# Where selection operations, gating, maximum passes and reciprocals stand in VectorE's stream

## The chip, the cores and the metric

One core of a Trainium2 chip runs the whole kernel. TensorE multiplies matrices, VectorE and ScalarE work on elements, GpSimd works on elements more slowly, SyncE issues the DMAs. Every engine runs its own list of instructions in the order in which the program wrote it; semaphores make one engine wait for another. The metric is the time of the whole program on the device in microseconds (us), as a median of several runs. A difference below some 0.2% can't be told from none.

## The reference

Two decoder layers over 1040 tokens (16 meta tokens and 1024 of the sequence, width 1024). A layer projects its input once, runs four branches of eight heads each, multiplies each by a gate, projects back and normalises:

```python
def hybrid_layer(x, ...):
    h = split_cols(x @ w_in)
    out_a = causal_dense_attention(qa, ka, va, key_valid, HEAD_DIM ** -0.5, decay)
    out_b = mla_attention(h['b_cq'], h['b_ckv'], h['b_kr'], ...)
    out_c = dsa_sparse_attention(...)      # keys chosen by an indexer
    out_d = sliding_window_sink_attention(...)
    mixed = jnp.concatenate([out_a * jax.nn.silu(h['a_g']), out_b * jax.nn.silu(h['b_g']),
                             out_c * jax.nn.silu(h['c_g']), out_d * jax.nn.silu(h['d_g'])], axis=-1)
    return layer_norm(ALPHA * x + mixed @ w_out, ln_g, ln_b)

def dsa_sparse_attention(...):             # for each block of 128 queries
    score = jnp.einsum('bqhk,bqh->bqk', jax.nn.relu(s), iwb) * IDX_HEADS ** -0.5
    _, idx = lax.top_k(jnp.where(adm, score, NEG), 256)
    # softmax attention over the 256 chosen keys alone
```

All arithmetic is in float32.

## The kernel before, in words

**Tiling.** Queries go in nine blocks: block 0 holds the 16 meta tokens, blocks 1 to 8 hold 128 tokens each. Block `i` sees `keys_of(i)` = 16 + 128 i keys: 1040 for block 8, 912 for block 7, 272 for block 2. Heads go in pairs, `p` = 0 to 3 in each branch. The order of a layer is an indexer stage, then branches A, D, B, C with four pairs each, then the output stage. Below, "pair A1" is pair 1 of branch A, and **step** `idx` of a pair works on block 8 - `idx` (the list `ORDER`, line 31), so step 0 is the largest block and step 8 the smallest. There are 2 x 16 x 9 = 288 steps.

**The plan.** The class `Plan` writes one list of items, and each engine goes through this one list and emits its own share of each item. So the order in which `pair` (line 318) adds items is the order of every engine's work; there is no other scheduler. A step adds, in this order: `tri` or `near` (GpSimd prepares the mask of the last chunk, A and C only), `rec` of the step before (`normalise`, line 386), `qk` part 0 (scores of this step's first two chunks), `pv` with the values of a block pair (`values`), `tp` of the step two before (`probabilities`, transposes), `qk` part 1 (third chunk), `exp` for the first head, `top` (line 395), `gt` (`gated`, line 396), a tile of projection work, `tp` for the second head, `exp` for the second head, and more projection work.

**What the items do.**
- `qk`: TensorE writes a chunk of scores for both heads into PSUM banks of `ps_s` (L980, in B also the rotary part, L991). VectorE's **maximum pass** (L1362) adds mask or bias, writes the row to `arena` and keeps the negative maximum in `nmax`; its end (semaphore `max_done`) frees the banks. Two pairs of banks, 0/1 and 2/3, take turns (`next_slot`).
- `exp`: ScalarE turns the row into exponentials and adds them up (L1148).
- `rec`: VectorE takes the **reciprocal** of the sums (L1374; in D, L1373 adds the sink first), then GpSimd multiplies the row by it (L1457, `nrm_done`). VectorE waits here for both exponentials of the step.
- `tp`: TensorE transposes the probabilities (L1003) into two banks of `ps_t`; ScalarE copies them out (L1159), and in C VectorE copies every other group (L1326).
- `pv`: TensorE multiplies values (L1015) into the single bank `ps_o`, in steps 1, 2, 4, 6 and 8.
- `gt`: VectorE's **gating** (L1382) multiplies `ps_o` by the gate tile, frees `ps_o` (`o_free`), and SyncE stores the result. VectorE waits here for `pv_done`.
- `mt` with what = "G", in steps 0 to 2: a chunk of the next gate tile. TensorE (L936) writes bank `P_BANK` = 4, ScalarE takes tanh (L1116) once `o_free` says that the old gate has been read, VectorE multiplies (L1299) and frees the bank. Other `mt` chunks are copied by ScalarE (L1109, L1112).
- `qb` (L945): a chunk of B's next queries, also in bank 4. For the rotary ones (what = "R") VectorE runs a chain of four instructions (L1312, L1314, L1316, L1317) before the bank is free. They fall in steps 6 and 7 (two in 7) of B0 to B2, and in steps 7 and 8 of D3.
- `kb` (L951): the three chunks of B's keys, added by `k_latent` in step 8 of D3 and of B0 to B2; ScalarE copies them (L1120).
- `top`: **selection operations** of VectorE on the indexer's scores, `TOP_OPS` = 448 per layer: for each block 8 down to 2, 64 operations over its whole row. They alternate: a maximum of eight (`MAX8`, L1193) and a replacement of these eight (`MATCH_REPLACE8` after `MATCH_VALUE_LOAD`, L1195). After the last of a block L1199 and L1200 make the mask. C needs all masks. `TOP_RATE` (line 43) says how many a step takes: 5 in A, 3 in D, 4 in B. That makes 432; the other 16 are done by line 1339, in the VectorE part, ahead of the first maximum pass of C.

```python
if br == "C" and it["p"] == 0 and it["idx"] == 0:
    top_ops(TOP_OPS)
```

Of the kernel before, what the change touches and what calls it, by code (L numbers as in the profile page):

```python
# [35 lines left out]
P_BANK = 4  # L36
# [3 lines left out]
Y_PARTS = [(0, 2), (2, 4), (4, 6), (6, 8), (8, 10), (10, 16)]  # L40

W_OUT_SETS = [4, 3, 3, 3, 3]
TOP_RATE = {"A": 5, "D": 3, "B": 4, "C": 0}


def keys_of(i):
    return N_META + BLK * i
# [6 lines left out]
def rows_of(b):  # L54
    return N_META if b == 0 else BLK
# [9 lines left out]
def score_chunks(br, i):  # L65

    if br == "D":
        return [(0, min(keys_of(i), 2 * BLK))]
    n = keys_of(i)
    if br == "C":  # L70
        tail = n if i <= 2 else 2 * BLK
        main = n - tail
        return (even(main, 1 if main <= 512 else 2) if main else []) + [(main, tail)]
    if br == "B":
        return [(0, 512), (512, 512), (1024, 16)] if n > 1024 else even(n, 2 if n >= 272 else 1)
    return even(n, -(-n // 512))
# [60 lines left out]
class Plan:  # L137
# [101 lines left out]
                for what in "NR" for c in range(3)]  # L239

    def k_latent(self, l, p):
        for c, bank in enumerate((P_BANK, 0, 2)):
            self.add("kb", l=l, p=p, cols=CHUNKS[c], **self.group("act", bank))

    def layer(self, l):
# [72 lines left out]
    def pair(self, l, br, p, nxt):  # L318

        fill = {}  # L320
        put = lambda idx, work: fill.setdefault(idx, []).append(work)
        for idx, work in enumerate(self.tile(l, "G", br=br, p=p)):
            put(idx, work)
        if br == "A":
            if p + 1 < NP:
                rest = self.tile(l, "AQ", p=p + 1) + self.tile(l, "AK", p=p + 1)
            else:
                rest = self.tile(l, "K", br="D") + self.tile(l, "Q", br="D", p=0)
            for idx, work in zip((3, 4, 5, 6, 7, 7), rest):
                put(idx, work)  # L330
        elif br == "D":
            if p + 1 < NP:
                for idx, work in zip((3, 4, 5), self.tile(l, "Q", br="D", p=p + 1)):
                    put(idx, work)
                for idx, b in zip((6, 7, 8), range(3 * p, 3 * p + 3)):
                    put(idx, lambda b=b: self.token_block(l, "TB", b))
                    if b:
                        put(idx, lambda b=b: self.latent(l, b - 1))
            else:
                put(0, lambda: self.latent(l, NB - 1))  # L340
                put(0, lambda: self.add("uw", l=l))
                work = [lambda b=b: self.token_block(l, "VB", b) for b in range(NB)]
                for idx, fn in zip((3, 3, 4, 4, 5, 5, 6, 6, 7, 4, 5, 6, 7, 8, 8), work + self.q_latent(l, 0)):
                    put(idx, fn)
                put(8, lambda: self.k_latent(l, 0))
        elif br == "B":
            if p + 1 < NP:
                for idx, work in zip((3, 4, 5, 6, 7, 7), self.q_latent(l, p + 1)):
                    put(idx, work)
                put(8, lambda: self.k_latent(l, p + 1))  # L350
            else:
                rest = self.tile(l, "K", br="C") + self.tile(l, "Q", br="C", p=0)
                for idx, work in zip((3, 4, 5, 6, 7, 7), rest):
                    put(idx, work)
        elif p + 1 < NP:
            for idx, work in zip((3, 4, 5), self.tile(l, "Q", br="C", p=p + 1)):
                put(idx, work)
        else:

            yy = self.take("yy")  # L360
            self.y_parts = self.y_half(l, ORDER[0], yy, 0) + self.y_half(l, ORDER[0], yy, 1)
            put(5, lambda: self.add("yl", l=l, b=ORDER[0], yy=yy, ln=None))
            for idx in (7, 8):
                put(idx, lambda: self.y_parts.pop(0)())

        hu = 8 * l + (p if br == "D" else 4 + p) if br in "CD" else None
        for idx, i in enumerate(ORDER):
            st = self.take("st")
            chunks = []
            for c0, w in score_chunks(br, i):  # L370
                g = self.take("chunk")
                bank = self.next_slot()
                chunks.append(dict(c0=c0, w=w, bank=bank, g=g,
                                   waits=self.banks([bank, bank + 1], ("max_done", 2 * (g + 1)))))
            row = (NB - 1 - i) % 3
            owner = self.row_owner[row]
            n = min(keys_of(i), 2 * BLK) if br == "D" else keys_of(i)
            s = dict(l=l, br=br, p=p, i=i, st=st, idx=idx, n=n, M=rows_of(i), chunks=chunks, row=row,
                     rwaits=latest([owner] if owner else []), a=(i + 1) // 2, hu=hu,
                     ds=self.take("ds") if br == "D" else None, tri=self.take("tri") if br == "A" else None,  # L380
                     nb=self.take("nb") if br == "C" else None)
            if br == "A":
                self.add("tri", **s)
            if br == "C":
                self.add("near", **s)
            self.normalise()
            self.add("qk", part=0, **s)
            self.values()
            self.pending.append(s)
            old = self.pending.pop(0) if len(self.pending) > LAG else None  # L390
            self.probabilities(old, 0)
            if len(chunks) > 2:
                self.add("qk", part=1, **s)
            self.add("exp", e=0, **s)
            self.add("top", l=l, count=TOP_RATE[br])
            self.gated()
            work = fill.get(idx, [])
            for fn in work[:1]:
                fn()
            self.probabilities(old, 1)  # L400
            self.add("exp", e=1, **s)
            for fn in work[1:]:
                fn()
            self.rec_next = s
        return None
# [49 lines left out]
def latest(events):  # L455
    out = {}
    for name, v in events:
        out[name] = max(out.get(name, 0), v)
    return sorted(out.items())
# [1098 lines left out]
```

## Time and profile before

| what | value |
|---|---|
| median of 3 runs | 3426.13 us (3424.23 to 3426.8) |
| the profiled execution | 3431.51 us, its span 3429.6 us |
| granted TensorE clock, mean | 0.964 of full speed |
| TensorE (PE) busy | 3117.4 us, 91% |
| VectorE (DVE) busy | 1701.0 us, 50% |
| ScalarE (ACT) busy | 1023.9 us, 30% |
| GpSimd (POOL) busy | 549.2 us, 16% |

"Busy" is the time in which an engine executes; an engine that is not busy waits for a semaphore or has nothing to do. The chain that ended last, followed back from the end, is made of the output stage's matmuls (L1029) for 6% of the span. In the trace an instruction stands with its start from the beginning of the span; TensorE's weight loads (PEld) run beside its matmuls. A float32 matmul is recorded as two instructions.

### The profile page before, as it was taken

Reading aid. Unit: us, or ns where it says so; the run is one execution under the profiler, and the core shown is the slowest. Engines: PE = TensorE matmul, PEld = TensorE weight load, DVE = VectorE, ACT = ScalarE, POOL = GpSimd, SP = SyncE. Lnnn points to the kernel's source line nnn. Section 1 sums busy time; section 2 is a strip of 40 time slices with the busy share of each in tenths; the row PEclk is TensorE's granted clock in tenths of the full one; section 3 lists DMA queues with packets and bytes.
Section 4 is the critical chain, followed back from the end, with each engine's and each line's share of the span. In section 5 each row is a group of like instructions: output and inputs, shape, how many; then the busy total and the mean of one; then the engine's idle time right before and its main releaser. Section 6 shows DMA issues by size and latency. Waiting matters only on the chain. (4 is left out here: it accounts for less than half of the span.)

```text
span 3429.6 us, 39909 instructions
## 1 busy us (share of the span) xinstructions
PE 3117.4 (91%) x14214; PEld 1769.8 (52%) x14214; DVE 1701.0 (50%) x4511; ACT 1023.9 (30%) x2757; POOL 549.2 (16%) x994
## 2 busy tenths in 40 slices
PE   4999999999799989989998998899998989899898
PEld 3445555555455555544443455555554555555443
DVE  4225877755566543432121268777555664443222
ACT  1223333334334323320002233333434443233100
POOL 0000222111111123320000012221111111333100
PEclk8999999999899999999999999999999999999999
DMA  5000110110000002032210001101110000120321
GB/s 210 27 25 26 38 38 28 35 36 28 32 15 20 15 27 93 19 128 67 74 59 21 25 31 38 38 28 36 35 42 19 15 15 19 31 87 13 117 74 61
DMA packets 91003, 153.04 MB, mean 45 GB/s; under 512 B 12656, under 2 KB 68224, under 8 KB 88504
## 3 DMA queue, kind: packets, MB, share of 16 engines
q1 hardware_dynamic: 90808, 150.50, 13.3%
q8 instruction: 115, 1.88, 0.2%
q14 instruction: 80, 0.66, 0.1%
HBM read 120.36 MB, written 32.21 MB: 44 GB/s over the span
## 5 line engine op out<-in xcount | busy, mean ns | idle before, releaser
L936 PE MATMUL ps_s<-xT,w_ring 128*128 128x348 f32 (+2 forms) x3616 | 1154.9, 474 | 11.0 <-DVE gate L1299 8.6
L936 PEld LDWEIGHTS ps_s<-xT,w_ring 128*128 128x128 f32 x3616 | 685.8, 195 | 415.0 <-issue 125.6
L1457 POOL TENSOR_SCALAR arena<-arena,small 128x256 f32<-128x256 f32 (+9 forms) x576 | 361.2, 638 | 1667.4 <-DVE small L1374 1663.2
L1148 ACT ACTIVATE arena<-arena,small 128x256 f32<-128x256 f32 (+9 forms) x576 | 380.2, 660 | 261.8 <-DVE small L1362 261.2
L1003 PE MATMUL ps_t<-ident,arena 128*128 128x128 f32 (+2 forms) x2432 | 361.0, 277 | 67.4 <-ACT arena L1159 49.6
L1159 ACT ACTIVATE arena<-ps_t 128x512 f32<-128x512 f32 (+4 forms) x700 | 309.4, 471 | 367.7 <-PE ps_t L1003 359.1
L1193 DVE MAX8 small<-score 128x8 f32<-128x1040 f32 (+6 forms) x448 | 377.3, 842 | 10.2
L980 PE MATMUL ps_s<-feat 64*128 64x256 f32 (+12 forms) x1888 | 318.9, 440 | 63.3 <-DVE small L1362 57.9
L1003 PEld LDWEIGHTS ps_t<-ident,arena 128*128 128x128 f32 (+2 forms) x2432 | 256.0, 132 | 228.2 <-issue 100.4
L1195 DVE MATCH_REPLACE8 score<-small,score 128x1040 f32<-128x1040 f32 (+6 forms) x448 | 369.8, 825 | 0.0
L1015 PE MATMUL ps_o<-arena 128*64 128x256 f32 (+3 forms) x2816 | 316.9, 362 | 31.5 <-ACT arena L1159 13.6
L1029 PE MATMUL ps_s<-arena,feat 128*128 128x512 f32 (+1 forms) x680 | 304.0, 600 | 10.2 <-DMA arena<-in_w_out 10.2
L1015 PEld LDWEIGHTS ps_o<-arena 128*64 128x64 f32 (+1 forms) x2816 | 181.9, 138 | 165.7 <-issue 55.9
L980 PEld LDWEIGHTS ps_s<-feat 64*128 64x128 f32 (+1 forms) x1888 | 150.8, 185 | 181.5 <-DVE small L1362 79.1
L1029 PEld LDWEIGHTS ps_s<-arena,feat 128*128 128x128 f32 (+1 forms) x680 | 126.5, 187 | 176.0 <-issue 163.8
L1232 DVE SCALAR_TENSOR_TENSOR arena<-score,ps_s 128x512 f32<-128x512 f32 (+1 forms) x34 | 23.3, 686 | 381.7 <-PE ps_s L1029 346.8
L906 PE MATMUL ps_s<-arena,xT 128*128 128x272 f32 (+3 forms) x576 | 202.4, 506 | 9.1 <-DMA arena<-in_w_tc 4.2
L1374 DVE RECIPROCAL small<-small 128x2 f32<-128x2 f32 (+1 forms) x288 | 46.8, 162 | 259.8 <-ACT arena L1148 256.2
L1288 DVE SCALAR_TENSOR_TENSOR score<-arena,small,score 128x1040 f32<-128x1040 f32 (+6 forms) x98 | 88.0, 901 | 175.6 <-ACT arena L1133 169.7
L906 PEld LDWEIGHTS ps_s<-arena,xT 128*128 128x128 f32 (+1 forms) x576 | 103.6, 185 | 96.7 <-issue 78.0
L1299 DVE SCALAR_TENSOR_TENSOR gate<-gate,ps_s 128x348 f32<-128x348 f32 (+1 forms) x96 | 49.3, 513 | 202.0 <-ACT gate L1116 202.0
L1116 ACT ACTIVATE gate<-ps_s 128x348 f32<-128x348 f32 (+1 forms) x96 | 44.1, 459 | 334.5 <-PE ps_s L936 268.5
(125 smaller groups left out, 2361.2 us busy)
## 6 DMA issues: line engine op xcount, KB each, us to landing
w_ring<-in_w_feat SPq DMA_DIRECT2D x78, 512.0 KB, 3.5
mixed<-mixg SPq DMA_DIRECT2D x128, 128.0 KB, 1.7
feat<-mixed SPq DMA_DIRECT2D x16, 1024.0 KB, 6.7
resid<-score SPq DMA_DIRECT2D x16, 512.0 KB, 3.1
score<-resid SPq DMA_DIRECT2D x16, 512.0 KB, 7.5
arena<-in_w_out SPq DMA_DIRECT2D x4, 1536.0 KB, 8.0
cT<-falls SPq DMA_DIRECT2D x8, 520.0 KB, 4.8
feat<-falls SPq DMA_DIRECT2D x8, 520.0 KB, 5.3
```

The costliest lines, as they stand in the source:

```text
L906: mm = pe.matmul(ps_s[0:M, bank, 0:n], xT[:, k, cols], wv[:, k, :], start=(k == 0), stop=(k == KT - 1))
L936: mm = pe.matmul(ps_s[:, bank, 0:w], w_ring[:, wt % 2, k, :], xT[:, k, c0:c0 + w], start=(k == 0), stop=(k == KT - 1))
L980: mm = pe.matmul(ps_s[0:M, ch["bank"] + e, 0:ch["w"]], q[r:r + HD, qc], k[r:r + HD, k0 + ch["c0"]:k0 + ch["c0"] + ch["w"]], start=True, st ...
L1003: mm = pe.transpose(ps_t[0:w, tg % 2, c * BLK:c * BLK + M], p_row(it, h, k0, w), ident[0:M, 0:M])
L1015: mm = pe.matmul(ps_o[HD * e:HD * e + HD, at:at + w], v_of(br, p, e, kb), arena[0:rows_of(kb), src:src + w], start=(j == 0), stop=(j == le ...
L1029: mm = pe.matmul(ps_s[0:M, bank, :], mix_in[slot][:, k, 0:M], w_out[k][:, cols], start=(k == 0), stop=(k == 15))
L1148: nc.scalar.activation(p, p, ACT.Exp, scale=-1.0, bias=nm[:, e:e + 1], accum_out=psums[0:M, st % 4, e:e + 1]).then_inc(S["exp_done"], 1)
L1159: a = nc.scalar.activation(dst, src, ACT.Copy)
L1193: dve.max(top8, sc).then_inc(S["top_step"], 1)
L1195: dve.match_replace(sc, top8, sc, TAKEN).then_inc(S["top_step"], 1)
L1288: dve.scalar_tensor_tensor(sc, src, w, sc, ALU.mult, ALU.add).then_inc(S["acc_done"], 1)
L1457: nc.gpsimd.tensor_scalar(p, p, rinv[0:M, st % 4, e:e + 1], 1.0, ALU.mult, ALU.mult).then_inc(S["nrm_done"], 1)
```

## The change

It has four edits, all in the plan.

1. `TOP_RATE` becomes a list with a number for each step. A pair takes 38 operations in A (before 45), 36 in D (before 27), 38 in B (before 36). In A and B step 8 takes 1.
2. `gated` is called ahead of `top`: in VectorE's stream the gating stands before the step's selection operations instead of behind them.
3. `qk` part 0 is added ahead of `normalise`: in VectorE's stream this step's first maximum passes stand before the reciprocal of the step before.
4. `k_latent` writes its first chunk to the bank pair that the scores used longer ago, the second to bank 4, the third to the other pair. Before: bank 4, 0, 2.

```diff
-TOP_RATE = {"A": 5, "D": 3, "B": 4, "C": 0}
+TOP_RATE = {"A": [3, 4, 5, 5, 6, 4, 5, 5, 1], "D": [4, 4, 4, 4, 4, 4, 4, 4, 4],
+            "B": [4, 4, 5, 5, 5, 5, 5, 4, 1], "C": [0] * 9}
...
     def k_latent(self, l, p):
-        for c, bank in enumerate((P_BANK, 0, 2)):
+        free = 2 * self.slot
+        for c, bank in enumerate((free, P_BANK, 2 - free)):
             self.add("kb", l=l, p=p, cols=CHUNKS[c], **self.group("act", bank))
...
                 self.add("near", **s)
+            self.add("qk", part=0, **s)
             self.normalise()
-            self.add("qk", part=0, **s)
             self.values()
...
             self.add("exp", e=0, **s)
-            self.add("top", l=l, count=TOP_RATE[br])
             self.gated()
+            self.add("top", l=l, count=TOP_RATE[br][idx])
             work = fill.get(idx, [])
```

## Rows read from the trace of the kernel before

**Rows 1.** The page, part 1: busy us, share of the span, instructions of an engine.
```profile
PE 3117.4 (91%) x14214; PEld 1769.8 (52%) x14214; DVE 1701.0 (50%) x4511; ACT 1023.9 (30%) x2757; POOL 549.2 (16%) x994
```

**Rows 2.** Waits of TensorE over the whole run: for whom, us, times, longest.
```profile
PE ps_s L980 <- DVE small L1362: 57.9, 29, 9.4
PE ps_t L1003 <- ACT arena L1159: 49.6, 97, 3.3
PE ps_s L945 <- DVE feat L1317: 29.2, 10, 4.5
PE ps_t L1003 <- DVE arena L1326: 17.6, 26, 1.9
```

**Rows 3.** Windows, steps 0 to 3: six pairs of A, C1, and A0 of layer 1.
```profile
core 0: us, PE busy (x) PEld busy (x) DVE busy (x) ACT busy (x) POOL busy (x), PEclk, DMA share, GB/s
396.70:442.60 45.90, 37.20 (x157) 22.29 (x156) 40.87 (x82) 15.44 (x34) 9.78 (x16) 0.89 0.13 41
...
sum 267.10, PE 219.94 PEld 132.12 DVE 226.37 ACT 92.58 POOL 58.68; mean PE 36.66 PEld 22.02 DVE 37.73 ACT 15.43 POOL 9.78
...
1309.60:1344.80 35.20, 33.12 (x165) 20.50 (x164) 16.53 (x61) 12.43 (x26) 12.11 (x16) 1.00 0.46 179
2012.40:2049.10 36.70, 30.93 (x136) 18.32 (x134) 35.37 (x73) 14.49 (x29) 9.27 (x14) 1.00 0.18 58
```

**Rows 4.** Groups of VectorE instructions in A1's stretch: busy, mean ns.
```profile
L1193 DVE MAX8 small<-score 128x8 f32<-128x1040 f32 (+1 forms) x12 | 14.8, 1232 | 0.3
L1195 DVE MATCH_REPLACE8 score<-small,score 128x1040 f32<-128x1040 f32 x11 | 13.5, 1226 | 0.0
...
L1195 DVE MATCH_VALUE_LOAD score<-small,score 128x8 f32 x11 | 1.0, 91 | 0.3
```

**Rows 5.** Timeline of TensorE in pair A1, idle time and its releaser in brackets.
```profile
401.84 1.52 PE L980 MATMUL ps_s<-feat 64*128 64x344 f32 x4 [3.73 <-DVE small L1362]
...
421.34 0.29 PE L1015 MATMUL ps_o<-arena 16*64 16x16 f32 x4 [2.20 <-ACT arena L1159]
```

**Rows 6.** Waits over the whole run, ScalarE's for the gating.
```profile
ACT gate L1116 <- DVE mixg L1382: 66.0, 12, 6.2
```

**Rows 7.** Windows, step 0 of C0 and of C1, layer 0.
```profile
1232.40:1251.60 19.20, 9.83 (x35) 5.58 (x34) 11.19 (x39) 2.69 (x7) 3.29 (x6) 0.73 0.07 20
1309.60:1317.80 8.20, 7.56 (x35) 4.42 (x34) 3.80 (x14) 2.29 (x7) 1.89 (x4) 1.00 0.90 348
```

**Rows 8.** Timeline of TensorE in the first step of C0.
```profile
1243.36 1.23 PE L980 MATMUL ps_s<-feat 64*128 64x256 f32 x4 [9.37 <-DVE small L1362]
```

**Rows 9.** Waits over the whole run, VectorE's before reciprocal and gating.
```profile
DVE small L1374 <- ACT arena L1148: 256.2, 149, 7.5
...
DVE mixg L1382 <- PE ps_o L1015: 32.1, 18, 3.5
```

**Rows 10.** Timeline of VectorE in pair B1, steps 6 and 7.
```profile
1056.25 0.57 DVE L1193 MAX8 small<-score 128x8 f32<-128x400 f32 x1
...
1059.60 0.52 DVE L1312 SCALAR_TENSOR_TENSOR rtmp<-ps_s,rope_t 64x348 f32<-64x348 f32 x1 [0.49 <-PE ps_s L945]
```

**Rows 11.** Timelines of TensorE in pair B1 (steps 6, 7) and pair D3.
```profile
1054.63 3.17 PE L1015 MATMUL ps_o<-arena 128*64 128x256 f32 x28
...
1066.79 2.15 PE L945 MATMUL ps_s<-cT,vw 128*128 128x344 f32 x4 [3.13 <-DVE feat L1317]
...
922.51 3.83 PE L951 MATMUL ps_s<-cT,vw 128*128 128x348 f32 x6 [2.04 <-DVE feat L1317]
```

**Rows 12.** Groups of selection instructions by shape, rows 400 wide, whole run.
```profile
L1193 DVE MAX8 small<-score 128x8 f32<-128x400 f32 x64 | 36.8, 575 | 1.1
...
L1195 DVE MATCH_REPLACE8 score<-small,score 128x400 f32<-128x400 f32 x64 | 35.8, 559 | 0.0
```

**Rows 13.** Windows: stage D of layer 0, and steps 4 to 8 of A1.
```profile
662.00:927.00 265.00, 238.06 (x1050) 140.35 (x1048) 154.50 (x451) 105.36 (x368) 44.91 (x110) 0.96 0.11 35
442.60:483.10 40.50, 39.49 (x211) 25.11 (x210) 28.75 (x58) 14.12 (x40) 9.31 (x20) 1.00 0.06 20
```

## The prediction

> **What bounds the kernel now.** I read the page's first part before anything else: TensorE is busy for 3117 of 3430 us [rows 1]. Nothing that only moves VectorE work can shorten those 3117 us, except where TensorE ran them at its lower clock; the change can win the idle time between matmuls and the slow matmuls beside it. The second view is who TensorE waits for [rows 2]: for VectorE's maximum passes (57.9 us), for ScalarE's copies of transposed probabilities (49.6 us), for the rotary chain that empties the one projection bank (29.2 us), for VectorE's own transposed copies (17.6 us). The third view cuts the run into equal pieces of work. Steps 0 to 3 (blocks 8 to 5) of a head pair have nearly the same matmuls in branch A and in branch C, but only A has selection operations between them. Six such stretches of A (pairs A1 to A3 in both layers) take 267.1 us, 44.5 each, at a granted clock of 0.89 in the first; the one of C takes 35.2 us at 1.00 [rows 3]. So A's first four steps are where VectorE sets the pace.
>
> **Why A is slow.** Two chains show in pair A1. Step 8 gives TensorE 3 us of work and VectorE five selection operations of 1.28 us (one maximum 1.232, or a load 0.091 and a replacement 1.226 [rows 4]). They run into the next pair, its first maximum pass is late, and TensorE stands 3.73 us before its third chunk [rows 5]. Then in steps 1 and 2 ScalarE's tanh may not overwrite the gate tile before VectorE's gating instruction has read it, and that instruction is behind five selection operations: ScalarE waits 66.0 us in 12 places for it [rows 6], its copies come late behind the tanh, and TensorE waits 2.20 us at the head of step 2 [rows 5]. The engine then works at half its clock (1.2 instead of 2.4 GHz) for a while: 0.89 is the mean over the stretch, and C's stretch without those stops is at full clock [rows 3]. The Trainium skill says the same of such gaps (TensorE: Matmul & The Clock Gate, HAM oscillation); by that rule a removed stop gives back more than its own length, and the trace agrees (0.89 against 1.00).
>
> **Part 1, A's steps 0 to 3.** With step 8 down from 5 operations to 1, step 0 from 5 to 3, step 1 from 5 to 4, and the gating ahead of them, both chains go. What is left is C's time: six stretches are 6 x 35.2 = 211.2, so 267.1 - 211.2 = 55.9 us. Pair A0 has no previous pair; its stretch is 36.7 us with 30.93 busy [rows 3], 5.8 idle, of which I leave 2.3 (first maximum pass and copies): 3.5 per layer, 7 in all. That makes 63. Against it: in A0 and A1 the rows are 1040 wide and VectorE is nearly full. The stretch of A1 has 40.87 us of VectorE work with 23 selection instructions [rows 3, 4]; 17 remain, so 40.87 - 6 x 1.28 = 33.2 us in a stretch of 35.2. I charge 1.5 us for each of these four pairs for being late, 6 us, and take **-57 us**; the bounds are -63 and half, -30.
>
> **Part 2, start of C.** The 16 left-over operations stood, whole, ahead of C's first maximum. The first step of C0 takes 19.20 us with a TensorE stop of 9.37 us [rows 7, 8], the same step of C1 8.20 us [rows 7]; both layers have the same order there, so I count it twice. The new rates add up to 4 x (38 + 36 + 38) = 448, all there are, so none is left, and the mask is ready one step before. 2 x 11.0 = **-22 us**. The cover of those 16 is B and D, below; bounds -22 and -19.
>
> **Part 3, gating ahead of selection: a new wait.** VectorE can now stand before the gating until TensorE has finished the value matmuls, with the selection operations, the gate product or the rotary chain and the next maximum queued behind. The trace of before has this wait only 18 times, 32.1 us [rows 9], since five operations covered it. In A and C nothing urgent is behind. In B, steps 6 and 7, there is: each rotary chain frees the bank for the next query chunk. In B1 the maximum ends at 1056.25, where selection starts; the value matmuls run until 1054.63 + 3.17 = 1057.80, so the gating ends at 1058.2 [rows 10, 11]. Five operations (now 5, not 4) of 0.64 us follow (0.575 for a maximum, 0.091 + 0.559 for a replacement, some 0.03 between them [rows 4, 12]): 3.2 us, so the chain starts at 1061.4 instead of 1059.60 and TensorE's stop of 3.13 us [rows 11] grows, with the one before it, by about 2.0. B0 pays 1.5 (its rows in step 7 shrink from 528 to 400), B2 1.3 (272 wide). 4.8 per layer is 9.6, and I add 3 for a half clock that lasts longer after these stops (the first such stretch of A shows that stops and low clock go together). **+13 us**, bounds 0 and +20. In D, 4 operations instead of 3 are 36 x 0.8 = 29 us per layer in a stage of 265 with 154.5 of VectorE busy [rows 13]: hidden, 0, bounds 0 and +4; if that cover were gone, 58 us. In A's later steps (4 to 8, 40.50 us with 28.75 busy) the waits are hidden likewise [rows 13]. The Trainium skill has a rule against this part (TensorE: Matmul & The Clock Gate, Architectural detail: the array is 16× 32×32, not 1× 128×128): VectorE's queue is strictly first in, first out. By it nothing behind the gating can pass its wait; the trace agrees, as a late gating holds ScalarE's tanh up for 66.0 us while selection runs [rows 6]. If all those waits reached TensorE, it would be the slower rival below.
>
> **Part 4, maximum ahead of the reciprocal.** The reciprocal waits for ScalarE's second exponential, 256.2 us in 149 places [rows 9]; the maximum no longer does. In C, where no selection covers it, the maximum and then VectorE's transposed copies come up to 1 us earlier; TensorE's waits for these are 17.6 us in all [rows 2]. I take a third, 5, and 1 for D3: **-6 us**, bounds 0 and -17.6. What is late next: GpSimd's normalising starts after the maximum (3.3 us at most), but its probabilities are transposed one step later, so no stop; its next bias sum in C queues behind it, in short steps only. ScalarE, SyncE and TensorE have neither reciprocal nor selection in their streams, so nothing else is moved past them, and no DMA.
>
> **Part 5, banks of the latent keys.** The first chunk no longer waits for the rotary chain, 2.04 us once per layer [rows 11], but the second does, and in D3 that chain comes about 1.3 us later (one operation more, and the gating). **0**, bounds -4 and +2.
>
> **Sum.** -57 - 22 + 13 - 6 + 0 = -72 us. The profiled execution took 3431.51 us (span 3429.6, 1.9 around it), 5.4 above the median 3426.13. 3431.5 - 72 = 3359.5 there, and 3354 us as a median.
>
> **Rivals.** *VectorE stays late in A.* 33.2 of 35.2 us leaves 2.0 for waits. If they are more, the 1040-wide pairs stay stretched and half of part 1 is lost: +28, 3382 us. For: the tanh and exponential waits stand in series with this work. Against: at 912 wide (A2, A3) there is room. *The rotary chains cost more.* If the stops of B and D3 double the low clock, part 3 is +20 to +30: 3366. *The stops of A are not these chains'*, so that only C's start comes: 3426 - 22 + 13 = 3417. Against: the releasers named in the rows. *Slower:* the wait before the gating, up to 3.2 us in step 4 and 1.5 in step 6, with half-clock time behind it, is not hidden but pushes every maximum; with about 6.7 us for each of the 24 pairs of A, D and B it costs 161, less the 95 of other gains: 3492 us. It decides from 4 us a pair on. Against: 11.7 us of VectorE idle in A's steps 4 to 8 alone [rows 13].
>
> **How the numbers follow.** Forecast 0.70; VectorE late 0.12; rotary chains 0.10; only C's start 0.04; slower 0.04. Range: 3332 (part 1 whole, part 3 nothing, part 4 at -10) to 3390 (half of part 1, with part 3 at +20). About 0.2% is what a measurement of this kernel can tell from no change. Faster 0.94, same 0.02, slower 0.04.
>
> **What would show it.** After: the six stretches of A near 36 us at clock 1.00; ScalarE's wait for the gating near 0; C0's first step 8.2 us; TensorE's wait for the maximum about 20 us; its wait for the rotary chain up from 29 to about 39; VectorE's wait for the value matmuls up from 32 to over 100 us. The forecast is wrong if A's stretches stay above 39, or if stops of 3 us appear in D.

## The result and the profile after

| | before | after |
|---|---|---|
| median of 4 runs each, taken together | 3426.47 us | 3326.97 us (3320.94 to 3329.28) |
| ratio, 95% interval | 1 | 0.9695 (0.9677 to 0.9712) |
| the profiled execution, its span | 3431.51, 3429.6 us | 3328.77, 3326.8 us |
| granted TensorE clock, mean | 0.964 | 0.978 |

The changed kernel is 3.05% faster: 27 us more than the 72 forecast, and below the range that was given (3332 to 3390). In the changed file a line of the old one stands 4 further down (L980 is L984, L1362 is L1366, L1382 is L1386, L1317 is L1321).

The page after, part 1, against [rows 1]:

```profile
PE 3079.5 (93%) x14214; PEld 1750.7 (53%) x14214; DVE 1690.5 (51%) x4511; ACT 1021.2 (31%) x2757; POOL 551.1 (17%) x994
```

The instructions are the same in number on every engine. TensorE is busy 38 us less with the same instructions, so that is matmuls that run at the higher clock; the other 65 us of the 103 are idle time. Who TensorE still waits for, against [rows 2] (us, times, longest):

```profile
PE ps_s L949 <- DVE feat L1321: 35.7, 16, 4.2
PE ps_t L1007 <- ACT arena L1163: 34.6, 97, 0.6
...
PE ps_s L984 <- DVE small L1366: 24.4, 24, 1.5
PE ps_t L1007 <- DVE arena L1330: 15.6, 27, 1.5
```

The maximum passes went from 57.9 to 24.4 us with no stop above 1.5, ScalarE's copies lost their long stops (longest 3.3, now 0.6), and the rotary chain took first place, 35.7 us in 16 places instead of 29.2 in 10.

**Where the time went.** I cut both runs at the first score matmul of each branch. Rows: layer 0's branches A, D, B, C (C with the output stage), then layer 1's. Columns: stretch and its length, busy us of each engine, granted clock, DMA. Before:

```profile
315.20:662.40 347.20, 314.25 (x1556) 193.72 (x1554) 273.92 (x578) 120.65 (x300) 75.05 (x140) 0.95 0.11 36
662.40:926.90 264.50, 237.56 (x1046) 140.04 (x1044) 154.10 (x450) 105.35 (x368) 44.91 (x110) 0.96 0.11 35
926.90:1232.40 305.50, 282.37 (x1683) 170.00 (x1683) 174.51 (x595) 119.17 (x301) 49.30 (x70) 0.95 0.05 18
1232.40:2012.40 780.00, 735.88 (x2861) 382.42 (x2860) 230.21 (x610) 165.40 (x409) 101.92 (x166) 0.98 0.17 55
2012.40:2356.00 343.60, 310.21 (x1556) 192.24 (x1554) 273.50 (x578) 120.73 (x300) 75.05 (x140) 0.97 0.11 36
2356.00:2620.20 264.20, 237.53 (x1046) 140.25 (x1045) 154.18 (x450) 105.33 (x368) 44.91 (x110) 0.96 0.11 35
2620.20:2922.10 301.90, 278.80 (x1683) 168.56 (x1683) 174.50 (x595) 119.11 (x301) 49.31 (x70) 0.96 0.06 18
2922.10:3429.60 507.50, 462.54 (x1919) 247.73 (x1918) 164.18 (x509) 94.99 (x236) 100.31 (x162) 0.97 0.20 64
```

And after:

```profile
315.60:624.90 309.30, 298.63 (x1556) 185.88 (x1554) 246.77 (x540) 120.05 (x300) 75.14 (x140) 1.00 0.13 40
624.90:886.10 261.20, 235.39 (x1044) 138.79 (x1043) 184.96 (x498) 104.68 (x368) 44.68 (x108) 0.97 0.11 36
886.10:1192.60 306.50, 281.52 (x1682) 169.97 (x1682) 174.54 (x609) 119.56 (x301) 50.24 (x72) 0.95 0.06 18
1192.60:1958.80 766.20, 731.63 (x2859) 380.82 (x2858) 220.67 (x587) 165.34 (x409) 102.02 (x166) 0.99 0.17 56
1958.80:2269.90 311.10, 300.29 (x1558) 186.66 (x1556) 246.91 (x540) 120.21 (x300) 75.16 (x140) 0.99 0.12 40
2269.90:2528.20 258.30, 232.78 (x1044) 137.78 (x1043) 184.93 (x498) 104.63 (x368) 44.69 (x108) 0.97 0.11 36
2528.20:2834.50 306.30, 281.22 (x1682) 169.79 (x1682) 174.58 (x609) 119.53 (x301) 50.23 (x72) 0.95 0.06 18
2834.50:3326.80 492.30, 459.21 (x1919) 245.87 (x1918) 155.22 (x486) 94.05 (x236) 100.42 (x162) 0.99 0.20 66
```

Length less busy time is TensorE's idle time of a stage. The two layers together: A -70.4 us, D -9.2, B +5.4, C with the output stage -29.0; -103.2 in all, against -102.8 in the span. In A idle time falls from 33.0 to 10.7 us in layer 0 while VectorE does 27 us less there and 31 us more in D: the operations moved to where they are covered.

**A's first four steps**, against [rows 3]: the first of the six stretches and their sum, then C1's of layer 0 and A0's of layer 1, and the first step of C0 against [rows 7].

```profile
392.70:426.50 33.80, 32.42 (x159) 19.83 (x158) 32.29 (x70) 15.42 (x34) 9.77 (x16) 1.00 0.18 56
...
sum 202.50, PE 194.20 PEld 118.80 DVE 189.16 ACT 92.29 POOL 58.61; mean PE 32.37 PEld 19.80 DVE 31.53 ACT 15.38 POOL 9.77
```

```profile
1258.20:1293.20 35.00, 33.06 (x167) 20.52 (x166) 16.06 (x61) 12.43 (x26) 12.12 (x16) 1.00 0.47 181
1958.80:1994.00 35.20, 32.55 (x136) 19.14 (x134) 31.77 (x69) 14.47 (x29) 9.29 (x14) 0.95 0.17 61
1192.60:1200.80 8.20, 7.56 (x35) 4.42 (x34) 3.82 (x16) 2.75 (x7) 3.32 (x6) 1.00 0.16 48
```

Of the stops of A1 in [rows 5], the one of 3.73 us at the pair's start is down to 0.65, and the one of 2.20 is gone. A third, at the end of step 2, goes from 2.36 us to 0.31. In TensorE's timeline, before (the stop of 2.36) and after:

```profile
432.25 0.49 PE L1003 MATMUL ps_t<-ident,arena 128*16 128x128 f32 x2 [2.36 <-ACT arena L1159]
```

```profile
394.82 0.85 PE L984 MATMUL ps_s<-feat 64*128 64x344 f32 x4 [0.65 <-DVE small L1366]
417.68 0.39 PE L1007 MATMUL ps_t<-ident,arena 128*16 128x128 f32 x2 [0.31 <-ACT arena L1163]
```

Of the two waits named in [rows 6] and [rows 9], ScalarE's for the gating has vanished (all 96 waits of its tanh are now for TensorE's chunk, 316.0 us, where 84 of them were before, 268.5 us), and VectorE's for the value matmuls grew from 32.1 us in 18 places to:

```profile
DVE mixg L1386 <- PE ps_o L1019: 130.4, 74, 3.5
```

**B1, steps 6 and 7**, against [rows 10, 11]: VectorE's gating and the first rotary instruction, then TensorE's stops.

```profile
1015.27 0.42 DVE L1386 SCALAR_TENSOR_TENSOR mixg<-ps_o,gate 128x256 f32<-128x256 f32 x1 [1.61 <-PE ps_o L1019]
...
1018.78 0.52 DVE L1316 SCALAR_TENSOR_TENSOR rtmp<-ps_s,rope_t 64x348 f32<-64x348 f32 x1
```

```profile
1020.89 1.41 PE L949 MATMUL ps_s<-cT,vw 128*128 128x348 f32 x4 [1.91 <-DVE feat L1321]
1025.97 1.77 PE L949 MATMUL ps_s<-cT,vw 128*128 128x344 f32 x4 [3.12 <-DVE feat L1321]
```

VectorE stands 1.61 us before the gating, then the five operations run, and the chain starts 3.5 us after the gating's start. The second stop is the old one (3.13, now 3.12); a new one of 1.91 us stands ahead of it.

### The profile page after: what moved, and what is told of

Its sections match the earlier page's. It is cut to its first block and busy times, and to the rows that moved or that the text cites. A ratio compares the mean times of both kernels' runs of the same rounds, so it can differ in the third digit from the quotient of the medians.

```text
span 3326.8 us, 39909 instructions
## 1 busy us (share of the span) xinstructions
PE 3079.5 (93%) x14214; PEld 1750.7 (53%) x14214; DVE 1690.5 (51%) x4511; ACT 1021.2 (31%) x2757; POOL 551.1 (17%) x994
## 5 line engine op out<-in xcount | busy, mean ns | idle before, releaser
L940 PE MATMUL ps_s<-xT,w_ring 128*128 128x348 f32 (+2 forms) x3616 | 1139.5, 469 | 5.1 <-DVE gate L1303 2.4
L940 PEld LDWEIGHTS ps_s<-xT,w_ring 128*128 128x128 f32 x3616 | 677.0, 192 | 399.3 <-issue 104.5
L984 PE MATMUL ps_s<-feat 64*128 64x256 f32 (+12 forms) x1888 | 310.2, 430 | 29.2 <-DVE small L1366 24.4
L984 PEld LDWEIGHTS ps_s<-feat 64*128 64x128 f32 (+1 forms) x1888 | 146.8, 180 | 143.5 <-issue 70.2
L1366 DVE CUSTOM_DVE_ANT_0 arena<-ps_s,causal 128x512 f32<-128x512 f32 (+5 forms) x144 | 57.7, 437 | 164.9 <-PE ps_s L995 164.6
L1120 ACT ACTIVATE gate<-ps_s 128x348 f32<-128x348 f32 (+1 forms) x96 | 44.1, 460 | 316.0 <-PE ps_s L940 316.0
L1330 DVE COPY arena<-ps_t 128x384 f32<-128x384 f32 (+4 forms) x124 | 65.2, 528 | 142.6 <-PE ps_t L1007 142.3
```

The costliest lines, as they stand in the source:

```text
L940: mm = pe.matmul(ps_s[:, bank, 0:w], w_ring[:, wt % 2, k, :], xT[:, k, c0:c0 + w], start=(k == 0), stop=(k == KT - 1))
L984: mm = pe.matmul(ps_s[0:M, ch["bank"] + e, 0:ch["w"]], q[r:r + HD, qc], k[r:r + HD, k0 + ch["c0"]:k0 + ch["c0"] + ch["w"]], start=True, st ...
```

## The experiments

A stop is a stretch in which TensorE is idle, and half-clock time is time for which its granted clock is 0.5. Idle times are TensorE's between the cuts described above, layer 0 where none is named. A ratio is to runs of the kernel before on the same chip. Those had a median of 3431.1 to 3433.0 us beside the experiments (single runs from 3424 to 3440), against the 3426.5 of the first table, so a gain is best read from the ratio; where I give one in us it is against the median beside it.

**The edits one by one.** The kernel before with one edit each: the rates and nothing else,

```diff
-TOP_RATE = {"A": 5, "D": 3, "B": 4, "C": 0}
+TOP_RATE = {"A": [3, 4, 5, 5, 6, 4, 5, 5, 1], "D": [4] * 9, "B": [4, 4, 5, 5, 5, 5, 5, 4, 1], "C": [0] * 9}
```

> The kernel before with the new rates alone. Two chains (theory): the late first maximum of A's step 0 and the start of C go, the tanh that waits for the gating in A's step 2 stays. A's six step-0 stops of 2.4 to 3.7 us fall to 0.65, C0's first step falls from 19.2 to 8.1 us, the stops in A's step 2 (4.9, 4.6, 3.6 us) stay within 1 us. Time -45 to -60 us, about 3375. Load alone (rival: VectorE simply had too much to do, order is irrelevant): the stops of step 2 go too, since steps 0 to 2 have three operations fewer; -85 us or more, 3340.

the gating and nothing else,

```diff
-            self.add("top", l=l, count=TOP_RATE[br])
             self.gated()
+            self.add("top", l=l, count=TOP_RATE[br])
```

> The kernel before with the gating ahead of selection alone, old rates. Two chains: the stops of A's step 2 go (20 us a layer with the slow clock behind them), those of step 0 and of C's start stay; B's rotary chains come later by the wait for the value matmuls, +1 us in B1. Time -30 to -42 us, about 3390. Load alone: nothing moves by more than 5 us, since VectorE has the same work.

the maximum passes and nothing else,

```diff
-            self.normalise()
             self.add("qk", part=0, **s)
+            self.normalise()
```

> The kernel before with the maximum ahead of the reciprocal alone. Two chains: it touches neither; a few tenths in C's steps 1 and 2 and 0.7 us in D3, -2 to -8 us. Rival (the maximum's wait for the second exponential is what held A up): -20 us or more.

and the first two together:

> Rates and gating without the two other edits. If they add up, A is as in the changed kernel (309 us in layer 0) and the time is -88 to -96 us, 3334. If the four edits need each other (rival: with the reciprocal first, VectorE has no room in A's 1040-wide pairs), A keeps 5 us or more over that, and the time is above 3342.

| kernel | median us | gain us | ratio, interval | idle in A, layer 0 / 1 |
|---|---|---|---|---|
| before, beside the next four | 3431.13 | | 1 | 33.0 / 33.4 |
| rates | 3374.85 | 56 | 0.983 (0.9806 to 0.9854) | 23.4 / 23.6 |
| gating | 3420.6 | 11 | 0.9967 (0.9954 to 0.9979) | 28.2 / 28.6 |
| maximum | 3405.85 | 25 | 0.9921 (0.9894 to 0.9948) | 28.9 / 29.3 |
| rates and gating | 3342.67 | 88 | 0.9736 (0.9711 to 0.9762) | 12.0 / 12.2 |
| all (after), beside 3426.47 | 3326.97 | 99.5 | 0.9695 (0.9677 to 0.9712) | 10.7 / 10.8 |

The rates came out as expected. The gating alone missed: 3420.6 instead of 3390. The maximum passes alone gave 25 us, where 2 to 8 were expected; that is the rival's figure (20 or more), though A's large stops stayed: in A1 they are 3.75 and 1.98 us, where they were 3.73 and 2.20. In its trace the four branches of both layers lose 24.1 us: A 11.7 (8.1 of it idle, in layer 0 TensorE's waits for ScalarE's copies, 18.5 to 14.4 us), D 9.5, C 6.8, and B gains 3.9. The second trace of the kernel before has A 3.8 us shorter than the first, so the 11.7 are 8 to 12.

Rates and gating together came to what was expected of the two (88 to 96 us), but they are not the sum of what each gives alone: 56 and 11 us alone, 88 together. Pair A1 shows why. With the rates alone, the stop at the start falls to 0.85 us and those behind the gating stay, 0.92 us at the head of step 2 and 4.05 at its end, where 2.20 and 2.36 were (file lines one further down):

```profile
396.36 0.85 PE L981 MATMUL ps_s<-feat 64*128 64x344 f32 x4 [0.85 <-DVE small L1363]
...
423.95 0.59 PE L1004 MATMUL ps_t<-ident,arena 128*16 128x128 f32 x2 [4.05 <-ACT arena L1160]
```

With the gating alone it is the other way round: step 2's stops shrink to 0.85 and 0.31, and the stop at the start of the pair grows from 3.73 [rows 5] to 5.68.

```profile
404.46 1.52 PE L980 MATMUL ps_s<-feat 64*128 64x344 f32 x4 [5.68 <-DVE small L1362]
...
424.70 4.92 PE L936 MATMUL ps_s<-xT,w_ring 128*128 128x348 f32 x16 [0.85 <-DVE gate L1299]
```

VectorE's work is the same, so time that TensorE no longer loses in the middle of a pair leaves VectorE less time to work off its list; it is late at the next pair's start instead. That was then an idea, and the next kernel tests it.

**Is it the load?** The kernel before with the gating ahead, and four of the five operations of A's step 8 sent to D's step 8:

```diff
-TOP_RATE = {"A": 5, "D": 3, "B": 4, "C": 0}
+TOP_RATE = {"A": [5] * 8 + [1], "D": [3] * 8 + [7], "B": [4] * 9, "C": [0] * 9}
```

> The kernel before with the gating ahead of selection, and A's step 8 down from 5 operations to 1 (the 4 go to D's step 8, so that C's start keeps its 16). If the gating alone gained little because VectorE was still late by its load when a pair began, the step 0 stops of 5.68, 5.08 and 4.35 us shrink by four operations (4 x 1.28 = 5.1 us) to under 1 us, A's idle time goes from 28.2 us per layer to about 16, and the time from 3420.6 to 3385 or so. If the five operations in steps 0 to 3 are what keeps VectorE late, stops before the gate's chunk in step 2 take their place: idle about 24 us per layer and 3400 to 3410. If load has no part in it, it stays at 3418 to 3423.

3387.4 us (0.9858, 0.9841 to 0.9874), idle in A 16.9 us: the numbers that the expectation gave if VectorE was late by its load (3385, 16). In A1 the stop at the start went from 5.68 to 0.85 us; five operations in steps 0 to 3 leave 1.56 us in step 2.

```profile
399.38 0.85 PE L980 MATMUL ps_s<-feat 64*128 64x344 f32 x4 [0.85 <-DVE small L1362]
417.93 4.92 PE L936 MATMUL ps_s<-xT,w_ring 128*128 128x348 f32 x16 [1.56 <-DVE gate L1299]
```

So sixteen operations a layer, moved from the one step that could not cover them, release 33 us (3420.6 to 3387.4; 37 by the ratios). They cost something where they went: D's idle time rose from 27.7 to 32.9 us, 3.1 of it in D3, where they stand ahead of a rotary chain (its stop goes from 3.44 to 6.55 us). The move without the gating was not run, so this kernel does not say what each of the two is worth; the gating on top of the new rates is worth 32 us (3374.85 to 3342.67).

**How full may VectorE be?** The changed kernel with the same 38 operations a pair, more of them in steps 0 to 3 (23 instead of 17):

```diff
-TOP_RATE = {"A": [3, 4, 5, 5, 6, 4, 5, 5, 1], "D": [4, 4, 4, 4, 4, 4, 4, 4, 4],
+TOP_RATE = {"A": [5, 6, 6, 6, 3, 3, 4, 4, 1], "D": [4, 4, 4, 4, 4, 4, 4, 4, 4],
```

> The changed kernel with A's 38 operations dealt [5,6,6,6,3,3,4,4,1]: six more in steps 0 to 3, which at 1040 wide is 7.7 us more of VectorE work in a stretch that TensorE passes in 33.7. Theory of the prediction (what VectorE is over, TensorE loses): about 5 to 6 us in each of A0 and A1, 3 in A2 and A3 at 912 wide, with slow clock 40 us in all, 3367. Rival (two pairs of banks and two transposed steps in hand let VectorE be late by several us before TensorE stops): under 10 us, 3335.

3356.05 us (0.9785, 0.9766 to 0.9804), 29 us above the changed kernel: between the two expectations, 40 us and under 10, and nearer to the first. Idle in A 24.1 us. The place where it shows in A1 is not the maximum pass but VectorE's gate product, which has to free the projection bank for the next gate chunk:

```profile
420.19 4.92 PE L940 MATMUL ps_s<-xT,w_ring 128*128 128x348 f32 x16 [2.83 <-DVE gate L1303]
...
430.54 4.92 PE L940 MATMUL ps_s<-xT,w_ring 128*128 128x348 f32 x16 [1.64 <-DVE gate L1303]
```

TensorE's wait for L1303 is 28.0 us over the run here, 2.4 in the changed kernel; with 20 operations in these steps, in the kernel with the light step 8, it is 13.7 (L1299 there). The cover ends gradually between 17 and 23 operations.

**The gating's place in B.** The changed kernel with B's gating behind the selection, as it was:

```diff
-            self.gated()
+            if br != "B":
+                self.gated()
             self.add("top", l=l, count=TOP_RATE[br][idx])
+            self.gated()
```

> The changed kernel with the gating behind the selection again in B alone. Theory: B1's stop in step 7 (5.03 us) falls by the 1.6 us that VectorE waits for the value matmuls less nothing else, to 3.4; B2's likewise by 1, B0's by 0.5: -3 us a layer, -6 in all, 3321. Rival (the fifth operation of step 6 makes it): under 1 us a layer.

3321.74 us (0.9679, 0.9661 to 0.9697), 5 us below the changed kernel, 7 below its runs on the same chip (3328.59); the intervals of the ratios overlap, so the time alone does not show a gain; the idle time is the firmer reading. It falls in B from 25.0 to 21.8 us in layer 0 and from 25.1 to 23.2 in layer 1. The new stop of B1 (1.91) is down to 0.17, the old one stands at 3.12: this is the price of part 3 in B, 2 to 3 us of idle time a layer.

**Selection behind everything in those steps.** In steps 6 and 7 of B0 to B2 and 7 and 8 of D3 the operations go to the end of the step:

```diff
-            self.add("top", l=l, count=TOP_RATE[br][idx])
+            late = (br == "B" and p < NP - 1 and idx in (6, 7)) or (br == "D" and p == NP - 1 and idx in (7, 8))
+            if not late:
+                self.add("top", l=l, count=TOP_RATE[br][idx])
...
             for fn in work[1:]:
                 fn()
+            if late:
+                self.add("top", l=l, count=TOP_RATE[br][idx])
```

> The changed kernel with the selection of steps 6 and 7 of B0 to B2 and of steps 7 and 8 of D3 put behind the rotary chains, at the end of the step. Theory: the chains start when their matmuls end; TensorE's stop of 1.91 us before the second rotary chunk goes and that of 3.1 before the third falls to about 1.4, 3.6 us in B1, 8 in B's three pairs, 2 in D3: 10 a layer, 20 in all with a few us of slow clock, 3305. Rival (the stops of B are the chains' own length, not what stands ahead of them): under 5 us. A loss would mean that the maximum behind the selection is late instead.

It missed: 3325.15 us (0.969, 0.9672 to 0.9709) where 3305 was expected, B's idle time 1.5 us lower per layer. The first rotary chain starts in time now, but step 6's operations stand between it and step 7's, and TensorE's one remaining stop in B1 is 3.74 us. Behind one chain is ahead of the next.

**No selection beside the rotary chains.**

```diff
-            "B": [4, 4, 5, 5, 5, 5, 5, 4, 1], "C": [0] * 9}
+            "B": [6, 6, 6, 6, 6, 6, 0, 0, 2], "C": [0] * 9}
```

> The changed kernel with B's selection operations taken out of steps 6 and 7 and put in steps 0 to 5 (6, 6, 6, 6, 6, 6, 0, 0, 2; the pair still takes 38). If the operations queued ahead of the rotary chains make the stops of B (3.50, 5.03, 3.83 us in step 7), what is left of each is the chain between two rotary chunks of one step, about 1.6 us: 7.5 us less idle per layer, 15 in all, with the half clock behind the stops 20 to 25, so 3303 to 3312 us. The rival is that six operations in steps 0 to 5 make VectorE late there and the gain is given back: B's idle time stays at 25 us per layer and the time within 3322 to 3332.

3296.85 us (0.9601, 0.9586 to 0.9615): 30 us under the changed kernel, and below the 3303 that the first theory had for its lower end. Idle in B 25.0 to 17.8 us, its half-clock time from 28.1 to 6.8 (in layer 1 from 27.8 to 14.1). Each of B0 to B2 keeps one stop of 1.60 us, the wait for the chain between two rotary chunks of one step; six operations a step elsewhere cost nothing that shows.

```profile
1013.71 1.39 PE L949 MATMUL ps_s<-cT,vw 128*128 128x344 f32 x4 [1.60 <-DVE feat L1321]
```

**The rotary chunks one step apart**, in B and D3 and then in B alone, on top of that:

```diff
-                for idx, work in zip((3, 4, 5, 6, 7, 7), self.q_latent(l, p + 1)):
+                for idx, work in zip((3, 3, 4, 5, 6, 7), self.q_latent(l, p + 1)):
...
-                for idx, fn in zip((3, 3, 4, 4, 5, 5, 6, 6, 7, 4, 5, 6, 7, 8, 8), work + self.q_latent(l, 0)):
+                for idx, fn in zip((3, 3, 4, 4, 5, 5, 6, 6, 7, 3, 4, 5, 6, 7, 8), work + self.q_latent(l, 0)):
```

> As the one before, and the chunks of B's next queries stand one step apart where they are rotary: steps 5, 6, 7 in B0 to B2 instead of 6, 7, 7, and steps 6, 7, 8 in D3 instead of 7, 8, 8. If the rest of the stops is a rotary chain between two chunks of the same step, B's stops in step 7 go to under 0.5 us and D3's in step 8 (5.44 and 0.88 us) to about 3 together: some 8 us less idle per layer than the one before, so 3283 to 3295 us. The rival is that the chunks moved ahead wait for ScalarE's latents or for the bank's former user, and the stop only changes its place: then it stays within 5 us of the one before.

> The changed kernel with no selection operations in steps 6 and 7 of B and the rotary chunks one step apart in B alone, D3 as in the changed kernel. If the spreading's gain in B (3.7 us less idle per layer than without it) was given back in D3 and in the first step of B0 behind it, this kernel keeps it: B near 285 us per layer with 14.1 us idle, D with 25.8 us idle, and 3285 to 3292 us. The rival is that the half clock takes it anyway: 3294 to 3299 us, as both kernels before it.

3295.26 us (0.9591, 0.9576 to 0.9605) and 3295.18 us (0.9602, 0.9578 to 0.9627). In B the stop is gone and idle falls from 17.8 to 14.1 us in both; in D3 it moved to the latent keys' chunk (3.5 us). Yet neither can be told from the kernel without them. Stage B of layer 0, first with the chunks as they were, then spread in B alone:

```profile
884.20:1173.60 289.40, 271.63 (x1684) 165.31 (x1684) 174.42 (x607) 119.32 (x301) 50.01 (x72) 0.99 0.06 19
```

```profile
886.80:1175.40 288.60, 274.48 (x1682) 166.86 (x1682) 174.37 (x607) 119.54 (x301) 49.93 (x72) 0.98 0.06 19
```

3.7 us less idle, 2.85 us more in the same matmuls: the clock fell to half in the first steps of B0 and B1, where it had not with the stops in. In layer 1 the 3.6 us did come back as 4.1. That need not be the spreading's doing: in layer 1 the clock is at half in these first steps of B0 and B1 in both kernels. So the rival of the last kernel held as to its time, and the idle time as to its place.

**The banks.** The changed kernel with the old order of banks:

```diff
-        for c, bank in enumerate((free, P_BANK, 2 - free)):
+        for c, bank in enumerate((P_BANK, 0, 2)):
```

> The changed kernel with the latent keys' first chunk in bank 4 again. If the banks are worth what the prediction put them at (0, between -4 and +2), this kernel is within 2 us of the changed one (3325 to 3329 us) and TensorE's wait for the rotary chain at the latent keys' chunk goes from 1.8 us in all back to about 4. Then the 15.7 us between the kernel with rates and gating alone (3342.7) and the changed one belong to the maximum pass. The rival gives the banks those 15.7 us: then this kernel is at 3340 us or above.

3322.64 us (0.9672, 0.9657 to 0.9686), a little below the 3325 to 3329 that were expected and no slower than the changed kernel; the rival's 3340 is out. TensorE's stop before the latent keys is 2.04 us again instead of 0.88, 1.2 us of idle time a layer, and the total does not show it. What lies between this kernel and the one with rates and gating (3342.67, ratio 0.9736), 20 us by the medians and 17 between the spans of the two traces, is then the maximum passes'.

**The same again.** Both kernels once more, for second traces:

> The changed kernel once more. It tells which of the stretches at half clock are there again: if those of D and B (16 and 28 us in layer 0, 13 and 28 in layer 1) come back within one stretch each, the 9 us that D became shorter belong to the kernel; if they move, they are a matter of the run.

> The kernel before, as it is, for a second trace. If the -9.1 us of stage D that the sum did not have are an effect of the change, both stages of D stay within 1 us of 264.4 and 264.2 us here, 3 to 5 us above the 261.2 and 258.4 us of the changed kernel. If half-clock stretches fall in other places in each execution, the stages of D differ from 264.4 and 264.2 by 2 to 5 us with TensorE's idle time in them (26.9 and 26.7 us) unchanged within 0.3.

The changed kernel: 3328.59 us (0.9697), the profiled execution's span 3317.1 instead of 3326.8 us. Its idle time repeats within 0.3 us in seven of eight stages (in B of layer 0 23.4 instead of 25.0), but B of layer 0 is 6.7 us shorter, D 2.4 us shorter and A 1.7 us longer, mostly by half-clock time. The kernel before: D 264.5 and 264.1 us, as in its first trace, A of layer 0 343.3 instead of 347.2. So D's gain is an effect of the change (258.3 to 261.2 in the four stages D of the changed kernel, 264.1 to 264.5 in the four of the one before), and a difference of 2 to 7 us in one stage of one trace need not be.

The 1.6 us of idle time in that one stage are explained by the trace itself. In B1 the chain behind the new stop ends when VectorE is done, whatever TensorE does meanwhile. In the first trace the matmuls between the two stops began with 1.41 us and the next stop took 3.12 (rows above); in the second they ran at half clock and took up what was idle before. The next chunk starts 5.08 us after the first in both:

```profile
1014.18 2.66 PE L949 MATMUL ps_s<-cT,vw 128*128 128x348 f32 x4 [1.91 <-DVE feat L1321]
...
1019.26 1.40 PE L949 MATMUL ps_s<-cT,vw 128*128 128x344 f32 x4 [1.68 <-DVE feat L1321]
```

## Why the prediction was wrong, step by step

The waits and chains that the prediction named moved as it said; three terms of its sum had the wrong size: part 1 was 10 us too small, part 3 some 8 us too dear and part 4 some 13 us too small, which makes the 31 us. In part 4 the mechanism was short too, as the last of the three paragraphs shows. What came as named: the six stretches of A at 33.8 us and clock 1.00 (near 36 was named), the wait for the gating gone, C0's first step at 8.20, the wait for the maximum at 24.4 (about 20), for the rotary chain at 35.7 (39), VectorE's for the value matmuls at 130.4 (over 100). Against the profiled execution the sum missed by 30.7 us (3359.5 and 3328.8). By its terms, with the stages' changes as measured:

| term | forecast | measured |
|---|---|---|
| part 1, A's steps 0 to 3 | -57 | -67 (A's -70.4 without part 4's 3.2) |
| part 2, start of C | -22 | -22 |
| part 3, gating ahead of selection | +13 | +5.4 |
| part 4, maximum first | -6 | -19 (A 3, C 7, D 9), with part 5's share in D |
| part 5, banks | 0 | 1.2 of idle time a layer in D; in the time not to be told from 0 |

Part 4's share is read so. In A it is what the kernel with the old banks has less than the one with rates and gating alone, 3.2 us. In C it is what is left of the -29.0 after the -22 of part 2, 7 us; the edit alone took 6.8 there. In D it is the stages' whole change, and that is the least certain: the two stages of D together take 528.7 us before and 519.2 with this edit alone, but 524.6 with rates and gating, and with the edit added to these (old banks) 523.7; the changed kernel has 519.5 and, in its second trace, 518.8. So D's part is 1 to 9 us by which pair of kernels is taken, and no pair separates it from half-clock time that differs between two executions.

**Part 1 was undersized by the choice of the yardstick and by a charge.** I took C's stretch as A's floor. After the change the same stretch of C still takes 35.0 us and A's 33.8: C's has 8 recorded matmul instructions more (167 against 159), 0.6 us of busy time and 0.6 of idle. Against the 35.2 taken as the floor that is 8.7 us in six (211.2 and 202.5). And the 6 us charged for VectorE being late at 1040 wide did not come: A1's stretch is as long as A2's and A3's, with VectorE busy for 32.29 of 33.80 us. The load was judged rightly (33.2 of 35.2 forecast), its effect was not; the overloaded kernel shows that the edge is there, some operations further on. A0's term of 7 is 5.9: 37.9 to 33.5 us in layer 0, 36.70 to 35.20 in layer 1, where a half clock has come in (0.95 in its row). Without part 4's 3.2 these make the ten: 8.7 + 6 - 1.1 - 3.2.

**Part 3 was right where it was worked out and wrong where it was guessed.** B1's new stop is 1.91 us (about 2.0 forecast), B2's stops grew by 1.2 (1.3). B0's shrank by 0.95 (4.45 to 1.91 and 1.59), where 1.5 more was forecast: with the new rates block 4's last operations and the making of its mask are over before the rotary chains, not among them. And the 3 us for a longer half clock are not to be seen apart from the variation between two traces. The gating's place in B costs 5 us by the run without it. But B's +5.4 is the stages' whole change, and without the maximum edit the gating on top of the rates leaves B as long as it was (603.5 and 603.2 us in both layers, 0.8 more of it idle in each). In D, where nothing was charged, the stops before D3's rotary chunks grew from 0.98 and 3.44 us to 1.26 and 4.17; the second is the fourth operation's, as it is 4.19 with the rates alone. The sign that the prediction gave, stops of 3 us in D, could not tell anything: one stood there already.

**Part 4 is the largest miss.** I priced it by TensorE's waits for VectorE's copies, in C. That share came near the forecast, 7 us for 5, partly by luck: these waits shrank by 2.0 us only (17.6 to 15.6), and the rest is other waits and half-clock time. A had no term, and the edit alone takes 8 us of idle time out of it, of which rates and gating had left 1.4 a layer to win. D was put at 1 us. In D3's step 3 a stop before L901 (L905 after), the product that makes B's values, gets 0.71 us shorter: it waits for ScalarE's copy of the one before. Before and after:

```profile
883.32 1.10 PE L901 MATMUL ps_s<-vw,cT 128*128 128x512 f32 x2 [1.65 <-ACT arena L1065]
```

```profile
845.21 1.10 PE L905 MATMUL ps_s<-vw,cT 128*128 128x512 f32 x2 [0.94 <-ACT arena L1069]
```

Three quarters of a microsecond, which is what I had seen. What I had not asked is what the clock does behind it. Steps 4 to 7 of D3, before and after:

```profile
884.40:910.30 25.90, 20.85 (x87) 9.86 (x86) 13.68 (x43) 13.52 (x39) 3.72 (x8) 0.93 0.03 11
```

```profile
846.20:870.60 24.40, 19.35 (x87) 9.40 (x86) 16.73 (x51) 13.54 (x39) 3.75 (x8) 1.00 0.03 12
```

The idle time is 5.05 us in both, the matmuls 1.5 us faster, as the clock stays at full speed; in layer 1 it is the same. All traces bear this out: with the reciprocal first that stop is 1.65 to 1.72 us, and in 9 of 12 stages D (six traces) the clock is at half for a while in D3's steps 4 to 7; with the maximum first it is 0.94 or 0.95, and the clock is at full speed there in all 20 stages (ten traces). The kernel with the maximum first alone is among these, so this is the edit's. D fell by 3.3 and 5.9 us in the two layers, its idle time by 1.1 in each, and that is the banks': with the old ones it is 27.0 and 26.7 us, as in the kernel before. That the shorter stop is the cause of the clock staying up is the reading that fits; no kernel here varied that stop alone.

**What the sum did not have** is that the edits help one another. My terms were made for all edits together, so the sum was spared this. It bore on the experiments: what was expected of the gating alone came only once the load was off the short step.

The Trainium skill (TensorE: Matmul & The Clock Gate, HAM oscillation) says of gaps that they cost more than their length, and this case agrees in A (22.3 us less idle in layer 0, 37.9 us less time) and D; the spread rotary chunks are a place where removing 3.7 us of idle in layer 0 gave 0.8, and both layers' took no more than 2 us off the median.

## What to carry over

Before pricing an order of instructions, find the step whose work on the bottleneck engine is shortest and take the filler out of it; here four operations in a 3-us step held back the gain of the gating, which was worth 11 us alone and 32 on top of the new rates (gating and the move of the four operations together gave 46). Filler that sits near a chain which frees a single buffer should go to other steps and not to the other side of the chain: reordering took 1.5 us of idle time out of a layer, removing 7. When a similar stage serves as a floor, subtract its own extra instructions and its own stops first.

## What the hardware showed that I had not expected

The granted clock falls in other places in two executions of one kernel: spans of 3326.8 and 3317.1 us with TensorE's idle time in A, D and C the same within 0.3 us. Idle time per stage is the steadier reading for effects under 5 us, except where VectorE sets the time: there a matmul at half clock shortens the stop behind it (3.12 to 1.68 us in B1) and the stage is as long as before. And a full VectorE did not slow the kernel by being full: while it was busy for 32.3 of 33.8 us in A1's first four steps, TensorE stood 0.65 us for it, and 0.31 us for ScalarE.

The fastest versions here are the ones with no selection operations beside the rotary chains: 3296.85 us, ratio 0.9601 (0.9586 to 0.9615), against 0.9695 for the changed kernel.
